# Conditioned decoder trunk on one core: a bias as a 32nd product, and eight low-part subtractions moved from VectorE to GpSimd

## The reference, cut to what matters

```python
ga = u_val * jax.nn.sigmoid(u_glu)
ca, nba = causal_dwconv(ga, bufs_a[l], conv_a_w[l], conv_a_b[l])
ya = jax.nn.silu(layer_norm(ca, ln_a_g[l], ln_a_b[l]))
cb, nbb = causal_dwconv(u_rec, bufs_b[l], conv_b_w[l], conv_b_b[l])
hb, hlast = rg_lru(cb, None if hs is None else hs[l], w_gate_a[l], b_gate_a[l],
                   w_gate_x[l], b_gate_x[l], lru_lambda[l], reset_first)
yb = hb * jax.nn.gelu(u_y)
mix = jnp.einsum('bte,ed->btd', jnp.concatenate([ya, yb], axis=-1), w_out[l])
x = x + gt_m * mix
...
```

## Time and profile before

| | |
|---|---|
| median of 3 runs | 1313.67 us (1310.01, 1313.67, 1318.68) |
| profiled execution | span 1311.8 us; the page gives no other time for it |
| PE | busy 1198.0 us, 91% of the span |
| DVE, ACT, POOL | busy 57%, 32%, 26% of the span |
| DVE from 392.65 to 436.47 us | busy 40.28 of 43.82 us |
| POOL in the same stretch | busy 14.07 us, with its waits inside instructions |

### The profile page before, as it was taken

How to read it: one execution, slowest core, us unless ns; L and a number is a source line. 1 busy time by engine, 2 the same in 40 slices (tenths; PEclk the granted TensorE clock), 3 DMA queues, 4 the chain that set the end, 5 groups by cost and what they waited for, 6 DMA issues and landing times.

```text
span 1311.8 us, 16680 instructions
## 1 busy us (share of the span) xinstructions
PE 1198.0 (91%) x6175; PEld 1075.4 (82%) x6175; DVE 744.7 (57%) x868; ACT 416.3 (32%) x729; POOL 338.1 (26%) x193
## 2 busy tenths in 40 slices
PE   4667999999745899899999999999999999999996
PEld 3457999999524688898998998998998998988985
DVE  4471899999699544643544444534534535435356
ACT  4574333432655433440230230320320410310322
POOL 0014788653033010230220320320410410311200
PEclk9768999999966899999999999999999999999998
DMA  8404343332002510120120120210210300300102
GB/s 304 150 0 145 104 121 112 96 112 81 0 19 96 170 33 0 37 77 17 36 77 17 59 66 3 66 62 0 80 48 0 96 32 0 96 32 21 59 32 104
DMA packets 74597, 87.25 MB, mean 67 GB/s; under 512 B 3752, under 2 KB 53184, under 8 KB 74563
## 3 DMA queue, kind: packets, MB, share of 16 engines
q1 hardware_dynamic: 72384, 85.21, 20.5%
q10 hardware_dynamic: 2179, 1.61, 0.5%
HBM read 81.72 MB, written 5.08 MB: 66 GB/s over the span
## 4 chain that ended last, share of the span: by engine, by line
PE 85%; DVE 9%; ACT 4%; issue 2%; ACTq 1%; DMA 1%; DVEq 0%
PE ps L1275 15%; PE ps L1277 14%; PE ps L1276 14%; PE ps L1411 11%; PE ps L1412 11%; PE ps L1414 11%; PE ps L1230 2%; PE ps L1231 2%; PE ps L1418 1%; PE ps L1417 1%; DVE rec L1073 1%; PE ps L1238 1%; PE ps L1250 1%; ACT w_hi L552 1%; DVE w_lo L938 1%
## 5 line engine op out<-in xcount | busy, mean ns | idle before, releaser
L1275 PE MATMUL ps<-act_hi,w_hi 128*128 128x384 f32 (+1 forms) x1152 | 381.9, 331 | 15.1 <-DVE act_lo L931 10.5
L1277 PE MATMUL ps<-act_hi,w_lo 128*128 128x384 f32 (+1 forms) x1152 | 379.4, 329 | 0.0
L1276 PE MATMUL ps<-act_lo,w_hi 128*128 128x384 f32 (+1 forms) x1152 | 379.4, 329 | 0.0
L1275 PEld LDWEIGHTS ps<-act_hi,w_hi 128*128 128x128 f32 x1152 | 219.7, 191 | 18.6 <-ACT act_hi L514 8.8
L1276 PEld LDWEIGHTS ps<-act_lo,w_hi 128*128 128x128 f32 x1152 | 219.7, 191 | 1.7
L1277 PEld LDWEIGHTS ps<-act_hi,w_lo 128*128 128x128 f32 x1152 | 219.5, 191 | 0.0
L1132 DVE TENSOR_TENSOR ps<-ps,gt_p 128x1024 f32<-128x1024 f32 x72 | 88.7, 1232 | 227.4 <-PE ps L1414 225.2
L346 POOL TENSOR_TENSOR w_lo<-raw,w_hi 128x1024 fp32r<-128x1024 f32 x48 | 118.3, 2467 | 359.5 <-ACT w_hi L519 310.4
L346 POOL TENSOR_TENSOR wb_lo<-raw,wb_hi 128x1024 fp32r<-128x1024 f32 x36 | 91.8, 2560 | 433.3 <-ACT wb_hi L519 424.6
L1411 PE MATMUL ps<-wb_hi 128*128 128x512 f32 x512 | 199.4, 389 | 1.1 <-ACT gt_s L786 1.1
L1412 PE MATMUL ps<-wb_lo,wb_hi 128*128 128x512 f32 x512 | 199.2, 389 | 0.0
(11 more groups left out here) (209 smaller groups left out, 1325.4 us busy)
## 6 DMA issues: line engine op xcount, KB each, us to landing
raw_ada<-in_w_ada SPq DMA_DIRECT2D x32, 512.0 KB, 3.7
raw<-in_w_up SPq DMA_DIRECT2D x32, 512.0 KB, 4.1
raw<-in_w_down SPq DMA_DIRECT2D x32, 512.0 KB, 3.3
x<-in_x_prompt SPq DMA_DIRECT2D x16, 512.0 KB, 7.1
ada<-in_w_ada SPq DMA_DIRECT2D x4, 2048.0 KB, 11.4
raw<-in_w_in SPq DMA_DIRECT2D x16, 512.0 KB, 4.7
raw<-in_w_out SPq DMA_DIRECT2D x8, 512.0 KB, 3.3
out<-x SPq DMA_DIRECT2D x8, 512.0 KB, 2.6
```

Source lines behind the costliest of these rows:

```text
L1275: mm(out, wh, xh, start=(k == 0), stop=False)
L1276: mm(out, wh, xl, start=False, stop=False)
L1277: last = mm(out, wl, xh, start=False, stop=(k == KD - 1))
```

## The change

- `sample_taps` on POOL writes a 32nd value beside the 31 products, the bias, with a copy of 64 columns; the reduction on DVE adds 32 values instead of 31, and L1013 with the wait before it goes. The semaphore `conva_tap` counts 32 steps a tile instead of 33, and PE's first mean waits for `smp_sum` as well.
- The low parts of the four recurrent outputs go from DVE to POOL (`yb_lo`), with a semaphore of their own, `yblo_done`.
- The low parts of all eight pieces of `w_out` are made on POOL.

```diff
-                    last = pool.tensor_tensor(prod_v[:, slot, :, t, :], ga_s[:, j, :, t:t + KA],
-                                              caw_j[:, bass.ds(j, 1), :].broadcast_to([P, NB, KA]), ALU.mult)
-                last.then_inc(smp_ready, 1)
+                    pool.tensor_tensor(prod_v[:, slot, :, t, 0:KA], ga_s[:, j, :, t:t + KA],
+                                       caw_j[:, bass.ds(j, 1), :].broadcast_to([P, NB, KA]), ALU.mult)
+                pool.tensor_copy(smp_prod[:, slot, :, KA:KA + 1],
+                                 par[:, bass.ds(C_CAB + j, 1)].unsqueeze(1).broadcast_to([P, SMP, 1])).then_inc(smp_ready, 1)
...
+            def yb_lo(j):
+                pool.wait_ge(yhi_done, j + 1)
+                pool.tensor_tensor(act_lo[:, J + j, 0:SEQ], gel[:, j, 0:SEQ], act_hi[:, J + j, 0:SEQ].bitcast(F32),
+                                   ALU.subtract)
+                pool.tensor_tensor(stk[:, J + j, SMP:P], gel[:, j, SEQ:TOK], stk[:, J + j, 0:SMP].bitcast(F32),
+                                   ALU.subtract).then_inc(yblo_done, 1)
...
-            for k in range(0, KD, 2):
-                pool.wait_ge(lo_ready, W_OUT0 + k)
+            for k in range(KD):
                 lo(W_OUT0 + k, k % 2, wb_lo[:, k, :], wb_hi[:, k, :])
-            pool.wait_ge(lo_ready, W_OUT0 + KD)
+                if k in (2, 3):
+                    yb_lo(2 * (k - 2))
+                    yb_lo(2 * (k - 2) + 1)
...
-                dve.wait_ge(smp_sum, j + 1)
-                dve.tensor_scalar(out_s, out_s, bias, None, ALU.add).then_inc(conva_tap, 1)
...
             normalise(0)
-            w_out_lo(1)
             normalise(1)
             swish(0)
-            for j in range(J):
-                dve.wait_ge(yhi_done, j + 1)
-                dve.tensor_tensor(act_lo[:, J + j, 0:SEQ], gel[:, j, 0:SEQ], act_hi[:, J + j, 0:SEQ].bitcast(F32),
-                                  ALU.subtract)
-                dve.tensor_tensor(stk[:, J + j, SMP:P], gel[:, j, SEQ:TOK], stk[:, J + j, 0:SMP].bitcast(F32),
-                                  ALU.subtract).then_inc(ylo_done, 1)
-                if j == 1:
-                    w_out_lo(3)
             ya_lo(0)
             normalise(2)
-            w_out_lo(5)
             for c in range(1, NC):
                 swish(c)
                 ya_lo(c)
-            w_out_lo(7)
...
-                    pe.wait_ge(ylo_done, J + t // NC + 1)
+                    pe.wait_ge(ylo_done, t // NC + 1)
+                    pe.wait_ge(yblo_done, J)
```

More of the change, by code:

```diff
@@ L53 @@
 RB_W = RB_P + NB * RB_S
-STEPS_A = KA + 2
+STEPS_A = KA + 1
 EPS = 1e-6
@@ L125, in trunk @@
         stk = sb("stk", [P, KD, P], F32R)
-        rx = shared([("conv_a_below", [P, J, TOK], F32), ("smp_prod", [P, 2, SMP, KA], F32)],
+        rx = shared([("conv_a_below", [P, J, TOK], F32), ("smp_prod", [P, 2, SMP, KA + 1], F32)],
                     [("conv_a", [P, J, TOK], F32), ("gel", [P, J, TOK], F32)],
@@ L192, in trunk @@
                              "sig_done", "ya_done"))
-        yhi_done, ylo_done = sem("yhi_done"), sem("ylo_done")
+        yhi_done, ylo_done, yblo_done = sem("yhi_done"), sem("ylo_done"), sem("yblo_done")
         gt_mm, gt_cp = sem("gt_mm"), sem("gt_cp")
@@ L295, in _ @@
             sp.wait_ge(yhi_done, J + NC)
-            sp.wait_ge(ylo_done, J + NC)
+            sp.wait_ge(ylo_done, NC)
+            sp.wait_ge(yblo_done, J)
             for t in range(NT):
@@ L1288, in mean_a @@
                     pe.wait_ge(conva_tap, STEPS_A * J)
+                    pe.wait_ge(smp_sum, J)
                 mean(c, 2 + c, lambda j: conv_a[:, j, c * CH:c * CH + CW[c]], mean_done)
@@ L1429, in _ @@
                     pe.wait_ge(yhi_done, J + t // NC + 1)
-                    pe.wait_ge(ylo_done, J + t // NC + 1)
+                    pe.wait_ge(ylo_done, t // NC + 1)
+                    pe.wait_ge(yblo_done, J)
                 elif t == NT - 1:
                     pe.wait_ge(yhi_done, J + NC)
-                    pe.wait_ge(ylo_done, J + NC)
+                    pe.wait_ge(ylo_done, NC)
                 tile_product(t, 0 if t % 2 == 0 else 2, KD,
```

## The result

The changed kernel takes **1319.68 us** (median of 20 runs, 1314.82 to 1325.01) against 1313.44 us of the kernel before (20 runs, 1310.01 to 1326.54). The ratio is 1.0038, 95% interval [1.002, 1.0057]: 5.0 us longer (2.6 to 7.5), which is within 1%. The 5.0 is worked out from the ratio; the two medians are 6.2 apart. The forecast was 1321.0, in a range of 1313 to 1327, with 0.89 for "within 1%".

The account below looks back on a forecast made before the run. PE bounds most of the kernel; from the last recurrent output to piece 7, DVE and POOL taking turns do. The stretch's +8.5 and the bias's -1.2 gave +7.3 on 1313.67, so 1321.0 us, range 1313 to 1327.

Parts of the forecast that it names:

- What bounds the stretch: From last recurrent output to last `w_out` piece: DVE and POOL take turns, so moved work is not hidden; 4.8 to 9.3 longer.
- The rival with hidden work: In the stretch, DVE and POOL don't hold each other up; piece 7 2.8 us sooner, total 1309.7; chance 0.08.
- that with ACT's order alone: In the stretch, ACT's order and not the turns sets the end; no change there, total 1312.5; chance 0.06.
- The size of the stretch, +8.5: Last recurrent output to piece 7 of `w_out` grows by 8.5 us, a middle taken with 4.8 to 10.5 as ends.
- the two cases of the walk: Second `normalise` in the stretch: L1044 waits out POOL's whole queue, piece 7 10.0 later, or alternates with POOL, 7.1 later.
- Case (4): In the stretch L1044 and POOL alternate; L1044 ends by 410 to 413 and piece 7 comes 7.1 us later.
- The bias, -1.2: Convolutions to PE's gates: L1013 goes, convolution B ends 1.2 us sooner and the gates follow; ends -3.0 to +1.
- Convolution B 7.0 sooner: Without L1013, DVE reaches convolution B about 7.0 us sooner, at 302.0 instead of 309.01.
- Standing there 5.9: At the start of convolution B, DVE meets POOL's three subtractions and stands about 5.9 us.
- What else moves costs nothing: Around the output projection: x tile loads, added PE waits and POOL's next `w_up` pieces cost no time.
- the signs named: POOL busy 30 us or more, an L1053 of several us, piece 7 about 8 us later, gates about 1 us sooner.

Follow-up runs that it names:

- the low parts alone: Against the kernel before, only the recurrent and `w_out` low parts moved to POOL, the bias staying a DVE instruction: ratio 1.0044, +5.8 us.
- the square above: Four kernels with the new bias: low parts unmoved or moved, ratios 0.9975 and 1.0038; with pieces 6, 7 earlier on ACT, 0.9951 and 0.9999, against the kernel before.
- the quarters: The changed kernel with each 1024-column POOL subtraction in the stretch cut into four of 256 columns: ratio 1.0059 to the kernel before.

## Why the prediction was right, and where it was off

- *What bounds the stretch* was right: DVE and POOL take turns, and moved work is not hidden. The rival with hidden work would have given 1309.7; that with ACT's order alone 1312.5, and the low parts alone then 0 instead of +5.8. But the prediction weighed turns and order against each other, and the square above shows both: the order, at a chance of 0.06, was worth 5.3 to 5.7 us of the stretch.
- *The size of the stretch, +8.5*, is the term that was mis-sized: +6.0 in the changed kernel, +5.8 with the low parts alone. The step that was off is the middle taken between the two cases of the walk, because of L1013. Case (4), alternation, said 7.1, and the second `normalise` ended within it: 406.70, which is 411.5 on the clock of before, where the walk had 410 to 413. Alternation is what all standing DVE instructions of the stretch did, and the quarters show that DVE's turn comes after one instruction of POOL's. The kernel before had rows for it too, which the choice left out: in convolution B two of its instructions stood one after the other, each let in after one of two POOL subtractions (first and second row DVE, third POOL; clean, L988 takes 0.28 and L985 1.28):

```profile
316.53 2.42 DVE L988 SCALAR_TENSOR_TENSOR ga<-rec,par,ga  x1
318.87 3.38 DVE L985 SCALAR_TENSOR_TENSOR ga<-rec,par,ga  x1
315.39 5.78 POOL L355 TENSOR_TENSOR aw_lo<-raw_ada,aw_hi 128x1024 fp32r<-128x1024 f32 x2 [7.52 <-ACT aw_hi L541]
```

- By the Trainium skill, SBUF — State Buffer, section "SBUF: two separate sides", the pair of ports that DVE and POOL share is locked for a whole instruction. The trace of the stretch agrees (2.69 the longest L1053 beside whole subtractions, 0.885 beside quarters); at L1013 the trace differs from a turn after one (5.60, 5.60 and 5.64 for three instructions), whatever its form.
- *The bias, -1.2*, was right in kind and too small. Convolution B 7.0 sooner: 7.1 measured. Standing there 5.9: 5.2 measured. Together -1.9 in place of -1.2. What the step left out is PE's clock at the gates, -1.5 more in these executions: the 3.03 us of idle time were counted as the most that could be won, and not as what put PE to 1.2 GHz for the first products.
- The two errors point the same way (2.5 us lost too many, 2.2 won too few), so the three distances give +2.6 where the sum had +7.3, and +3.8 to the end of the span. The runs' +5.0 and +3.2 lie on either side of that. The forecast's own interval, 1315.5 to 1325.2, holds them all. That 1321.0 came within 1.3 us of the measured 1319.68 is in part luck: the two medians are 6.2 apart, where the ratio gives 5.0 and the traces 3.8.
- *What else moves costs nothing* held, and one clause of it shows its limit: the x tiles did not matter with piece 7 at 49.9 or at 43.9, and did once it came at 37.
- Of the signs named: POOL 36.99 us busy in the stretch (30 or more); L1053 of the second `normalise` 2.40 and 2.49, where one of several us was named; gates 1.9 sooner (about 1); piece 7 6.0 later, not about 8.

## What to carry to other kernels

An engine's busy share can hide that its work is standing: here DVE's rose by 4.5 us when 10.7 us of work were taken from it, because POOL takes twice the time for the same subtraction and DVE stands meanwhile. Before moving work between two engines that hold each other up, read which wait ends last on the chain; here it was the order on a third one, and changing that shortened the stretch by 5.3 to 5.7 us. Look also behind an idle gap of PE: what closes it can bring back the clock as well.

## What the runs showed of the hardware that was not expected

- A DVE instruction that meets POOL's subtractions is let in after one in every case of the stretch and of convolution B, and after three at one place, 5.60, 5.60 and 5.64 us in three kernels, with one input or two. The cause is open.
- The other way round it is not one for one: POOL stood until a whole run of DVE's instructions was through. In the kernel before, the subtraction of 6.38 us stood through the rest of one L1111 and four more, until 417.48. With all pieces on POOL and the recurrent parts on DVE one took 10.36 us (410.28 to 420.64), through the rest of one and nine more. So alternation, one instruction each, is shown for a waiting DVE and not for a waiting POOL. Why is open too. The two of POOL there (duration ns min/median/max, start us):

```profile
L346 POOL TENSOR_TENSOR wb_lo<-raw,wb_hi x2: 3719/7040/10362, 410.3 to 420.6; 128x1024 fp32r<-128x1024 f32 x2
```

- Cutting a subtraction of POOL in four costs 0.45 us by itself (2.80 for 2.35), and about as much again by the DVE instructions that get in between.
- PE's clock at the gates: 1.2 GHz (0.50) for the first 4 us after 3.14 us without work, mixtures (0.57 and 0.74) in two executions after 3.03, and 2.4 GHz (1.00) in all eleven executions with 1.12 to 1.15.
